# Attention of a fused transformer kernel: values and turned probabilities split into high and low parts, first head's weights prepared one stage earlier

## What is computed

```python
q = (c_q @ w_uq).reshape(B, T, 8, 128)
q_lat = einsum('bthd,hdc->bthc', q, w_uk) * 128 ** -0.5
# of each query's keys the 256 of the highest score are kept
logits = einsum('bqhc,bqkc->bqhk', q_lat, kv_sel) + bias
p = softmax(where(dist >= 0, logits, -inf))
o_lat = einsum('bqhk,bqkc->bqhc', p, kv_sel)
o = einsum('bthc,hcv->bthv', o_lat, w_uv)
```

## Time and profile before

| what | value |
|---|---|
| median of 3 runs | 2378.28 us (2377.05 to 2380.7) |
| profiled execution | 2377.78 us, of which 2375.9 us are the span from first to last instruction |
| mean granted TensorE clock | 0.944 |
| PE, PEld | 2209.5 us (93%), 1877.4 us (79%) |
| DVE, ACT, POOL | 1781.1 us (75%), 1136.8 us (48%), 421.4 us (18%) |
| `select_keys` | about 159 to 286 us of the span |
| `attention` | 287.8 to 552.0 us of the span |

### The profile page before, as it was taken

How to read it: one execution, slowest core, us unless ns; L and a number is a source line. 1 busy time by engine, 2 the same in 40 slices (tenths; PEclk the granted TensorE clock), 3 DMA queues, 4 the chain that set the end, 5 groups by cost and what they waited for, 6 DMA issues and landing times. The chain is left out here.

```text
span 2375.9 us, 31093 instructions
## 1 busy us (share of the span) xinstructions
PE 2209.5 (93%) x10909; PEld 1877.4 (79%) x10909; DVE 1781.1 (75%) x2931; ACT 1136.8 (48%) x1948; POOL 421.4 (18%) x418
## 2 busy tenths in 40 slices
PE   8989699998999999999999989789989999999996
PEld 5779688886887788887887979667878788788875
DVE  7699766665689987876789585573789987658797
ACT  5478655445353343334444563484553333554442
POOL 2122222222430122220001212003321111000002
PEclk9985599999999999999999999799999999999997
DMA  9014200004443332239431101002345534755431
GB/s 379 22 63 155 80 14 14 31 1 152 128 155 125 122 132 103 98 116 332 155 94 42 45 27 36 18 1 89 106 169 219 197 146 181 276 168 164 135 92 71
DMA packets 93097, 276.38 MB, mean 116 GB/s; under 512 B 11136, under 2 KB 15648, under 8 KB 89120
## 3 DMA queue, kind: packets, MB, share of 16 engines
q1 hardware_dynamic: 85472, 226.64, 28.5%
q10 hardware_dynamic: 7488, 47.98, 4.9%
HBM read 208.19 MB, written 66.39 MB: 116 GB/s over the span
## 5 line engine op out<-in xcount | busy, mean ns | idle before, releaser
L158 PE MATMUL banks<-f_hi,f_w_hi 128*128 128x512 f32 x608 | 238.0, 391 | 4.9 <-DVE f_w_lo L3884 3.6
L159 PE MATMUL banks<-f_lo,f_w_hi 128*128 128x512 f32 x608 | 237.2, 390 | 0.0
L160 PE MATMUL banks<-f_hi,f_w_lo 128*128 128x512 f32 x608 | 237.1, 390 | 0.0
L3415 ACT CAST f_w_hi<-f_raw 128x512 fp32r<-128x512 f32 x173 | 107.6, 623 | 256.0 <-PE banks L160 190.6
L1985 ACT CAST w_hi<-w_raw 128x512 fp32r<-128x512 f32 x152 | 94.1, 622 | 230.2 <-PE set L160 99.5
L158 PE MATMUL set<-gate_hi,w_hi 128*128 128x512 f32 x420 | 164.6, 392 | 4.0 <-issue 3.2
L159 PE MATMUL set<-gate_lo,w_hi 128*128 128x512 f32 x420 | 163.9, 390 | 0.0
L160 PE MATMUL set<-gate_hi,w_lo 128*128 128x512 f32 x420 | 163.9, 390 | 0.0
L158 PE MATMUL set<-b_hi,w_hi 128*128 128x512 f32 x384 | 150.9, 393 | 5.8 <-DVE w_lo L2315 5.8
L3095 POOL TENSOR_TENSOR f_w_lo<-f_raw,f_w_hi 128x512 fp32r<-128x512 f32 x64 | 95.1, 1488 | 335.3 <-ACT f_w_hi L3415 335.3
L160 PE MATMUL set<-b_hi,w_lo 128*128 128x512 f32 x384 | 150.4, 392 | 0.0
(11 more groups left out here) (577 smaller groups left out, 6129.7 us busy)
## 6 DMA issues: line engine op xcount, KB each, us to landing
gates<-x ACTq DMA_DIRECT2D x25, 1536.0 KB, 5.9
w_raw<-in_w_ff SPq DMA_DIRECT2D x53, 512.0 KB, 3.6
gate_raw<-gates SPq DMA_DIRECT2D x105, 256.0 KB, 2.8
f_gate_raw<-gates SPq DMA_DIRECT2D x70, 256.0 KB, 2.8
ada<-in_ada_w SPq DMA_DIRECT2D x32, 512.0 KB, 3.5
f_raw<-in_f_w_v SPq DMA_DIRECT2D x26, 512.0 KB, 3.5
f_raw<-in_f_w_u SPq DMA_DIRECT2D x25, 512.0 KB, 3.8
down_raw<-in_w_ff SPq DMA_DIRECT2D x18, 512.0 KB, 4.3
```

The costliest lines, as they stand in the source:

```text
L158: nc.tensor.matmul(out, w_hi, x_hi, start=start, stop=False)
L159: nc.tensor.matmul(out, w_hi, x_lo, start=False, stop=False)
L160: return nc.tensor.matmul(out, w_lo, x_hi, start=False, stop=stop)
L3415: nc.scalar.copy(w_parts(n)[0][:, :], source(n)).then_inc(w_hi_s, 1)
```

## The change

In `attention` both float32 products become three split ones.

- The value projection multiplies the high and low parts of c_kv (held anyway) by those of w_uv, so weights are split over all 768 columns and the sum of the parts of c_kv is not formed. ACT writes the values' high part and DVE, after it, the low part, in place of DVE's one copy.
- ACT's copy of `turned` writes the high part, `pt_hi`. A new DVE instruction per tile, `turned_low`, subtracts it from `turned` and writes `pt_lo`. It stands last in DVE's list for tile m, after normalize(m + 1). PE's two waits on `pt_s` (before turn(m + 1) and before times_v(m)) now wait for this instruction.
- The first head's weights: SP loads them at the head of `select_keys`, ahead of the modulation weights; ACT casts them after its last count there; POOL subtracts after its last step. In `attention` the two counters are set at once.

```diff
@@ select_keys
             def _(sp):
+                sp.dma_start(heads.raw[:, :], d["w_heads"][0]).then_inc(head_loaded, 16)
                 m.loads(sp)
...
                 for i in range(LAST):
                     count(i)
+                act.wait_ge(head_loaded, 16)
+                nc.scalar.copy(heads.hi[:, :], heads.raw[:, :]).then_inc(head_hi, 1)
                 act.wait_ge(rows_s, 2)
...
                     pool.sem_inc(next_s, 1)
+                pool.wait_ge(head_hi, 1)
+                then(nc.gpsimd.tensor_tensor(heads.lo[:, :], heads.raw[:, :], f32(heads.hi[:, :]), ALU.subtract))
@@ attention, SP
-                sp.dma_start(raw[:, :], d["w_heads"][0]).then_inc(w_loaded, 16)
@@ attention, POOL
-                    nc.gpsimd.tensor_tensor(w_lo[:, :], raw[:, 0:4 * P], f32(w_hi[:, :]), ALU.subtract)\
-                        .then_inc(w_lo_s, 1)
+                    nc.gpsimd.tensor_tensor(w_lo[:, :], raw[:, :], f32(w_hi[:, :]), ALU.subtract).then_inc(w_lo_s, 1)
...
-                for k in range(2):
-                    nc.gpsimd.tensor_tensor(ckv[:, k, :], f32(ckv_hi[:, k, :]), f32(ckv_lo[:, k, :]), ALU.add)\
-                        .then_inc(ckv_s, 1)
-                weights(0, 0)
+                pool.sem_inc(w_lo_s, 1)
@@ attention, PE
-                                mm = nc.tensor.matmul(ring[u % 2][:, j // 4, (j % 4) * P:(j % 4 + 1) * P],
-                                                      ckv[:, k, j * P:(j + 1) * P], w_v[:, k * P:(k + 1) * P],
-                                                      start=(k == 0), stop=(k == 1))
+                                s, ks = slice(j * P, (j + 1) * P), slice((4 + k) * P, (5 + k) * P)
+                                mm = three_products(nc, ring[u % 2][:, j // 4, (j % 4) * P:(j % 4 + 1) * P],
+                                                    ckv_hi[:, k, s], ckv_lo[:, k, s], w_hi[:, ks], w_lo[:, ks],
+                                                    k == 0, k == 1)
...
-                        mm = nc.tensor.matmul(out[qt // 4][:, (qt % 4) * P:(qt % 4 + 1) * P], proj_v[hh][:, s],
-                                              pt[qt % PT][:, s], start=(j == 0), stop=(j == qt))
+                        mm = three_products(nc, out[qt // 4][:, (qt % 4) * P:(qt % 4 + 1) * P], v_hi[hh][:, s],
+                                            v_lo[hh][:, s], pt_hi[qt % PT][:, s], pt_lo[qt % PT][:, s], j == 0, j == qt)
...
-                pe.wait_ge(ckv_s, 2)
@@ attention, ACT
-                    nc.scalar.copy(w_v[:, :], raw[:, 4 * P:6 * P])
-                    nc.scalar.copy(w_hi[:, :], raw[:, 0:4 * P]).then_inc(w_hi_s, 1)
+                    nc.scalar.copy(w_hi[:, :], raw[:, :]).then_inc(w_hi_s, 1)
...
+                    nc.scalar.copy(v_hi[hh][:, :].rearrange("p (a b) -> p a b", a=2), ring[u % 2][:, :, :])\
+                        .then_inc(v_hi_s, 1)
...
-                    nc.scalar.copy(pt[qt % PT][:, 0:w], turned[:, 0:w]).then_inc(pt_s, 1)
+                    nc.scalar.copy(pt_hi[qt % PT][:, 0:w], turned[:, 0:w]).then_inc(pt_hi_s, 1)
@@ attention, DVE
-                    dve.wait_ge(full, i * PER + (u + 1))
-                    nc.vector.tensor_copy(proj_v[hh][:, :].rearrange("p (a b) -> p a b", a=2), ring[u % 2][:, :, :])\
+                    dve.wait_ge(v_hi_s, i * 2 + (hh + 1))
+                    nc.vector.tensor_tensor(v_lo[hh][:, :].rearrange("p (a b) -> p a b", a=2), ring[u % 2][:, :, :],
+                                            f32(v_hi[hh][:, :]).rearrange("p (a b) -> p a b", a=2), ALU.subtract)\
                         .then_inc(free, 1)
...
+                def turned_low(i, hh, qt):
+                    dve.wait_ge(pt_hi_s, tile(i, hh, qt) + 1)
+                    w = (qt + 1) * P
+                    nc.vector.tensor_tensor(pt_lo[qt % PT][:, 0:w], turned[:, 0:w], f32(pt_hi[qt % PT][:, 0:w]),
+                                            ALU.subtract).then_inc(pt_s, 1)
...
                             normalize(i + 1, 0, 0)
+                        turned_low(i, m // QT, m % QT)
```

More of the change, by code:

```diff
@@ L170, with select_keys @@
 ROWS = QT - FIRST_SCORED
-def select_keys(c, d, score, mask):
+def select_keys(c, d, score, mask, heads):
     nc = c.nc
@@ L216, in select_keys @@
                                "tied", "penalties", "rows_made", "diag_masked"))
+        head_loaded, head_hi = c.sem("head_loaded"), c.sem("head_hi")
         m = Modulation(c, st, d, 16, 48)
@@ L407, in _, with __init__ @@
                     pool.sem_inc(next_s, 1)
+                pool.wait_ge(head_hi, 1)
+                then(nc.gpsimd.tensor_tensor(heads.lo[:, :], heads.raw[:, :], f32(heads.hi[:, :]), ALU.subtract))
+class HeadWeights:
+    def __init__(self, c, st):
+        c.sb_right(st, "wo_place", [P, 2 * KT * P])
+        self.raw = c.sb_right(st, "wh_raw", [P, 6 * P])
+        self.hi = c.sb_right(st, "wh_hi", [P, 6 * P], F32R)
+        self.lo = c.sb_right(st, "wh_lo", [P, 6 * P], F32R)
 class BiasWindows:
@@ L987, in front, with attention @@
     return cq_hi, cq_lo, ckv_hi, ckv_lo, mask, window, score
-def attention(c, d, cq_hi, cq_lo, ckv_hi, ckv_lo, mask, window, o, wo_raw):
+def attention(c, d, cq_hi, cq_lo, ckv_hi, ckv_lo, mask, window, o, wo_raw, heads):
     nc = c.nc
@@ L1006, in attention @@
     with ExitStack() as st:
[L1007 to L1011, removed]
+        raw, w_hi, w_lo = heads.raw, heads.hi, heads.lo
         proj_hi = [c.sb(st, f"proj_hi{b}", [P, 2, T], F32R) for b in range(2)]
         proj_lo = [c.sb(st, f"proj_lo{b}", [P, 2, T], F32R) for b in range(2)]
-        proj_v = [c.sb(st, f"proj_v{b}", [P, T]) for b in range(2)]
+        v_hi = [c.sb(st, f"v_hi{b}", [P, T], F32R) for b in range(2)]
+        v_lo = [c.sb(st, f"v_lo{b}", [P, T], F32R) for b in range(2)]
         near = [c.sb(st, f"near{i}", [P, 2 * P]) for i in range(NEAR)]
         prob = [c.sb(st, f"prob{i}", [P, T]) for i in range(PROBS)]
-        pt = [c.sb(st, f"pt{i}", [P, T]) for i in range(PT)]
+        pt_hi = [c.sb(st, f"pt_hi{i}", [P, T], F32R) for i in range(PT)]
+        pt_lo = [c.sb(st, f"pt_lo{i}", [P, T], F32R) for i in range(PT)]
         top_far, top, neg_top, total, inv = (c.sb(st, n, [P, QT]) for n in ("top_far", "top", "neg_top", "total", "inv"))
@@ L1023, in attention @@
             "wo_first_loaded", "wh_loaded", "wh_hi", "wh_lo", "ring_full", "ring_free", "proj_hi_done"))
-        near_s, far_top_s, neg_s, exp_s, inv_s, prob_s, turned_s, pt_s, pv_s, out_s, ckv_s = (
-            c.sem(n) for n in ("near_done", "far_top_done", "neg_top_done", "exp_done", "inv_done",
-                               "prob_done", "turned_done", "pt_done", "pv_done", "out_copied", "ckv_summed"))
+        near_s, far_top_s, neg_s, exp_s, inv_s, prob_s, turned_s, pt_hi_s, pt_s, pv_s, out_s, v_hi_s = (
+            c.sem(n) for n in ("near_done", "far_top_done", "neg_top_done", "exp_done", "inv_done", "prob_done",
+                               "turned_done", "pt_hi_done", "pt_lo_done", "pv_done", "out_copied", "v_hi_done"))
         order = [(0, "proj", n) for n in range(3)]
@@ L1179, in weights @@
                 def weights(i, hh):
-                    act.wait_ge(w_loaded, i * 32 + 16 * (hh + 1))
-                    nc.scalar.copy(w_v[:, :], raw[:, 4 * P:6 * P])
-                    nc.scalar.copy(w_hi[:, :], raw[:, 0:4 * P]).then_inc(w_hi_s, 1)
+                    act.wait_ge(w_loaded, i * 32 + 16 * hh)
+                    nc.scalar.copy(w_hi[:, :], raw[:, :]).then_inc(w_hi_s, 1)
                 def project(i, hh):
@@ L1190, in project @@
                             .then_inc(proj_hi_s, 1)
-                    act.wait_ge(full, i * PER + (place[hh, "proj", 2] + 1))
+                    u = place[hh, "proj", 2]
+                    act.wait_ge(full, i * PER + (u + 1))
+                    nc.scalar.copy(v_hi[hh][:, :].rearrange("p (a b) -> p a b", a=2), ring[u % 2][:, :, :])\
+                        .then_inc(v_hi_s, 1)
                     if hh == 0:
@@ L1229, in _ @@
                 act.sem_inc(out_s, HALVES)
-                weights(0, 0)
+                act.sem_inc(w_hi_s, 1)
                 for m in range(AHEAD):
@@ L4649, in build_program @@
                 cq_hi, cq_lo, ckv_hi, ckv_lo, mask, window, score = front(c, d, work, first, idx)
-                select_keys(c, d, score, mask)
+                with ExitStack() as early:
+                    wo_raw = [c.sb_right(early, f"wo_raw{i}", [P, KT * P]) for i in range(2)]
+                heads = HeadWeights(c, first)
+                select_keys(c, d, score, mask, heads)
             c.end_stage()
-            with ExitStack() as early:
-                wo_raw = [c.sb_right(early, f"wo_raw{i}", [P, KT * P]) for i in range(2)]
-            attention(c, d, cq_hi, cq_lo, ckv_hi, ckv_lo, mask, window, work, wo_raw)
+            attention(c, d, cq_hi, cq_lo, ckv_hi, ckv_lo, mask, window, work, wo_raw, heads)
         xs = c.sb(ctx, "x", [P, KT, T2])
```

## The result

| | median | lowest to highest |
|---|---|---|
| before (4 runs) | 2378.16 us | 2377.05 to 2380.7 |
| changed kernel (4 runs) | 2470.69 us | 2464.35 to 2489.26 |

The ratio is 1.040, 95% interval 1.034 to 1.046: slower, as forecast, but by 92 us where 62 were forecast, and beyond the top of the range (2462). The profiled execution of the changed kernel took 2465.6 us, with a span of 2463.8.

What follows compares the result with a forecast made beforehand. The prediction took attention to be bound by PE's own work and by waits where DVE's list is late. Profiled 2377.8 + 46.9 (loads) − 5.7 (start) + 21 (waits) = 2440 us, range 2409 to 2462.

Steps and rivals of the forecast that it cites:

- What bounds attention: In attention, PE's own work and places where DVE's list runs behind set the stage's 264 us.
- Part 1: Value projection and probability products: three products for one raise loads from 832 to 1248, +46.9 us on PE.
- cheap loads: Rival, chance 0.14: split products' loads in attention come nearer to the array's 0.06 us; about 2411 us.
- the other side: Rival, chance 0.04: faster than before, product at 0.18 us or less and low part hidden on DVE; about 2366.
- Part 3: Attention: the probabilities' low part on DVE makes PE wait before its transposes, +20 us of PE idle, 21 in the sum.
- written-out lists: Engine instruction lists for all 64 attention tiles, played through with priced durations; PE's waits per head pair: 5.6 old, 10.7 new.
- Part 2: Start of attention: PE begins near 288.0 instead of 293.75, −5.7 us, with the moved steps costed at nothing.
- The clock: Granted PE clock in attention: the sum gave its fall no cost, 0 us.
- falling clock: Rival, chance 0.15: clock falls at 8 head starts and projections instead of two places, 3.4 us each, +20 us, 2460.
- After attention: Stages behind attention: as long as before, 0 us.
- The range: Whole kernel, 8 in 10: 2409 to 2462 us, taking in most of the clock rival and part of the cheap-load one.

Runs made afterwards that it cites:

- e4: The changed kernel with times_v in float32 again and no turned_low, so only the value projection is split; 2388.0 us, ratio 1.004.
- e1: The changed kernel without turned_low: pt_lo zeroed once, ACT's copy signals PE directly, all 1248 loads kept; 2428.0 us, ratio 1.020.
- e2: The kernel before with turned_low added, writing a tile nobody multiplies, and PE waiting for it; products stay float32; 2409.3 us, ratio 1.013.
- e6: The kernel before with the first head's weights split in select_keys and POOL's subtraction there waiting for the first thresholds; 2370.4 us, ratio 0.9965.
- e3: The changed kernel with two matmuls per product in place of three, in values and times_v; 2428.1 us, ratio 1.021.
- the filler: The changed kernel with one 512-column matmul more per tile, ahead of the tile's logits; 2451.1 us, and 2450.9 us when repeated.

## Why the prediction was wrong, step by step

- *What bounds attention*: right. PE's own loads set the stage, and its idle time is where DVE's list is late.
- *Part 1, 46.9 us of loads*: right in mechanism and size. The changed kernel loads 416 times more, at 0.11 us; e4 gives 14.0 us where 14.6 were summed, and e1's stage fits 46.9 within what the clock leaves open. The rival cheap loads is out, and with it the other side. (The upper end of cheap loads was also added up wrong: 8 + 41 − 5.7 is 43, not 39; nothing rests on it.) The 81 ns of the Trainium skill ("TensorE: Matmul & The Clock Gate", section "Back-to-back issue gap"), by which part 1 would be an estimated 8 us, are not seen in these traces.
- *Part 3, the waits*: right in mechanism, the size was off: +14.0 in place of +21 us in the changed kernel, +26 in place of +38 in e2. The written-out lists reproduced the old waits and overstated the new by half. The low part's own durations came as priced (277 to 1225 ns), so the error is not there; which step of the lists makes it was not found.
- *Part 2, the start*: the gain was 3.6, not 5.7. The step that failed is "POOL's subtraction comes when POOL has no work ..., DVE may lose some tenths": it held a DVE instruction for 1.6 us, and with POOL's subtraction moved (e6) the instruction is back at 0.16. The rest is the 0.65 us by which the selection stage began later.
- *The clock*: this step failed and sank the forecast. The sum had the clock at nothing, and the rival falling clock had the right mechanism and even named the halved streaming, but was priced at 6 places x 3.4 = 20 us and given 0.15. Measured are 60 us more at 1.2 GHz and 25 us of time, in the second profile 92 and 40. The rival erred twice. It took 3.4 us, the length of the shorter spell of the earlier trace rows at the lower level, as the spell's price, which can be half of it at most; and it took all spells to be as short. Read in windows of 1 us, the kernel before has two spells behind the stage's opening, of 6.8 and 3.4 us, and the changed kernel six, of 3.4 to 20.5 us. Two of them:

```profile
466.00:487.00 21.00, 18.27 (x78) 0.52 0.06 19
616.00:634.00 18.00, 16.68 (x78) 0.52 0.00 0
```

  That the spells grew because the products between them stream half of the time is argued from e3 and the filler, not read from single spells. The rival's own condition, "the array streams only half of the time in a value product", was a reason to give it more than 0.15.
- *After attention*: forecast "as long as before", measured +5.5. The clock was still at 0.50 until 644 us, in the output product. In the first 60 us behind the stage that makes some 17 us at half against 10, which can cost 3 us. The second profile of the changed kernel has 1829.2; the other kernels' remainders lie between 1822.8 and 1827.6 us. So the clock can be a part of the 5.5; this was not tested.
- *The range*: its top, 2462, was 2 us above the rival's own 2460, so that it left no room for longer spells. The changed kernel's executions differ by 25 us (2464 to 2489), those of before by 4.

What stays open: why the clock falls at one place and not at another. Waits of the same length are followed by a fall in one head and not in the next: in the changed kernel's profile the clock falls at PE's wait of 1.90 us before 467.40, and stays at 1.00 at those of 1.91 before 382.71 and 1.89 before 552.98.

## What to carry to other kernels

Price a split product of 128 columns by its loads, not by its passes: three float32r matmuls cost 0.34 us where one float32 product costs 0.22, and they also leave the array idle for part of each load, which can take the clock of everything around them down. Where an instruction moves to POOL, the question is not only whether POOL is idle but which DVE instruction runs beside it: here a tensor_tensor with two SBUF inputs and the normalization were slowed, a count was not. Move the release of POOL's instruction past such a one, and look for a sign like the one here, a normalization that takes longer at 256 columns (915 ns) than at 512 (563 ns). A price taken from rows holds at one clock level, so a forecast for a stage near the edge needs both levels.

## What the runs showed of the hardware

- More work made a kernel faster: 64 matmuls of 512 columns took 19 us off, with 41 and 33 us at 1.2 GHz in place of 76 and 107.
- Neither halved streaming (22 us more at the lower level) nor waits (14 more) alone did what both did together (60 to 92 more).
- Two executions of one kernel spent 76 and 107 us of the same stage at the lower level, and the stage differed by 13 us.
- At the lower level weight loads are slower as well: the split products' matmuls start 0.21 in place of 0.11 us apart.
- A DVE instruction of three columns took 1.73 us beside a POOL tensor_tensor, while a DVE count with one SBUF input beside it took the same 0.74 us as alone.
